# Three gather buffers instead of two beside the gate spreading, and later token rows for the second set

## The chip, the cores and the metric

The kernel runs on one core of one Trainium2 chip. The metric is device time in microseconds (us) for one execution of the whole program, taken as the median of several runs. All arithmetic is in float32.

## The reference, cut to what matters

One layer of a decoder trunk is computed for 256 tokens of width 2048. A mixer comes first. The change touches what follows it, the PEER retrieval. For each token, 8 heads pick 16 experts each out of 16,384, and every expert is one row of a table `u` and one row of a table `v`:

```python
def block(args):
    xb, idb, gb = args                      # tokens, expert numbers, gates
    ub = jnp.take(u_tab, idb, axis=0)
    act = jax.nn.gelu(jnp.einsum('tkd,td->tk', ub, xb))
    vb = jnp.take(v_tab, idb, axis=0)
    return jnp.einsum('tk,tkd->td', (gb * act), vb)
```

So a token needs 128 dot products with rows of `u` and a weighted sum of 128 rows of `v`. Each table holds 128 MB.

## The kernel before

The 256 tokens are split. For the last 160 tokens the kernel works densely: it multiplies their rows with the whole of both tables, and an array `p0` of gates (zero for experts not picked) selects what counts. For the first 96 tokens it gathers only the rows that were picked.

**The dense part.** TensorE multiplies 128 chunks of `u` (1 MB each, ring `wraw` of four slots, loaded by SyncE; function `chunk`, line L511), ScalarE takes the gelu of each result into `act_u` (L1063), and after that TensorE multiplies 128 blocks of `v` (1 MB each, eight slots: `wraw` and `vmore`, `v_tile`, L794). A chunk or block is 16 matmuls of 160 columns. In the trace each of these matmuls shows as two records, so a chunk is `x32`.

**The gate spreading.** `p0` is built beside chunks 20 to 47 of `u`. For each group of four tokens, 40 groups in all, VectorE writes one-hot matrices (`one_hots`, L1512 and L1516) into a ring of three (`HOT_RING`), TensorE multiplies them (`spread`, L771), and ScalarE copies the result into `p0` (`gates_out`, L1093). A chunk has one spread in its middle, and 12 of the 28 chunks have a second one at their end. TensorE runs its program in order, so a one-hot matrix that is late holds up the chunks behind it.

**The gathered part.** The 96 tokens form three sets of 32. Each take gathers one row for each of 32 tokens times four picks, 128 rows of 8 KB, 1 MB in all, by an indirect DMA that GpSimd issues (L1650). VectorE then uses it: a `u` take multiplies it with the token rows `hrep[:, s]` and sums (L1527), a `v` take adds it, weighted, to `yacc` (L1538). There are 192 takes of 32 each, in the order u0, u1, v0, u2, v1, v2. Gather buffers are the tiles `gat`. Beside the spreading two are in use. The third and fourth lie where the dense part holds the activations until then, and open when six batches of weights are done (`s_p0`).

**Order on VectorE.** Beside the spreading, `S0_TAKES` takes are dealt evenly behind the 40 groups of one-hots. Then come 16 batches `weights(i)` (L1545), each of which waits for eight chunks of `u` and is followed by `U_TAKES[i]` takes. The remaining takes come beside the `v` blocks. From take `G2_TAKE` = 136 on, every third one is followed by `add_g2`, which multiplies one of 16 modulation tiles that ScalarE's queue loads. The fourteenth of those loads stands behind a wait for 90 `v` blocks.

**Token rows.** `hrep` holds for each set the 32 tokens' rows, four times over (8 KB in each of 128 partitions for a set). It is written by four DMAs from `hrow_dram` that GpSimd issues: two sets before the takes begin (L1636), the third set when the spreading is done (L1645), since the one-hots lie in its place until then.

Of the kernel before, what the change touches and what calls it, by code (L numbers as in the profile page):

```python
# [37 lines left out]
D = 2048  # L38
# [38 lines left out]
SET_T = P // REP  # L77
# [3 lines left out]
N_TAKES = len(TAKES) * SET_G  # L81
# [6 lines left out]
GT = 4  # L88
SPREADS = N0 // GT
HOT_RING = 3  # L90
S0_TAKES = 36
U_TAKES = (0, 1, 0, 1, 0, 4) + (7, 7, 7, 7, 7, 6, 6, 5, 4, 4)
V_TAKES = N_TAKES - S0_TAKES - sum(U_TAKES)
G2_TAKE = 136
Y_BANKS = tuple(range(2, 8))
# [34 lines left out]
def hybrid_block(nc, xT, xrow, fnorm, par, cst, mixc, shifts, relb, wmod, wst, lruw, subk, sel, utab, vtab, hrow_dram, rel_dram, res_dram, silu_dram, gain_dram, out):  # L130
    ctx = ExitStack()
    with ctx:
# [9 lines left out]
        def at(name, kb, shape, dt=F32):  # L142
            assert kb * 256 + int(np.prod(shape)) <= size, name
            return nc.alloc_sbuf_tensor_at(name, [P, *shape], dt, offset=base + int(kb * 1024))
# [92 lines left out]
        hot_a = at("hot_a", 189.5, [HOT_RING, GT, P])  # L237
        hot_b = at("hot_b", 213.5, [HOT_RING, GT, P])
        p0 = at("p0", 77.5, [NB, N0])
        gat = [at(f"gat{i}", kb, [D]) for i, kb in enumerate((197.5, 205.5, 61.5, 69.5))]  # L240
        vmore = [at(f"vmore{i}", kb, [D]) for i, kb in enumerate((45.5, 53.5, 157.5, 165.5))]

        csil_back = at("csil_back", 77.5, [D])
# [78 lines left out]
        def v_slot(m):  # L322

            j = m % V_RING
            return row_of(wraw, (N_U + j) % W_RING) if j < W_RING else vmore[j - W_RING][:]

        def gather_slot(g):

            if g < S0_TAKES:
                return g % 2, (g // 2 + 1) * 16, (g - 2 if g >= 2 else None)  # L330
            slot, turn = (g - S0_TAKES) % 4, (g - S0_TAKES) // 4
            if slot < 2:
                return slot, (S0_TAKES // 2 + turn + 1) * 16, (g - 4 if turn else g - 2)
            return slot, (turn + 1) * 16, (g - 4 if turn else None)

        def taken(g):

# [19 lines left out]
        s_m0 = [sem(f"first_mod_loaded{i}") for i in range(M_RING0)]  # L357
        s_m = [sem(f"mod_loaded{i}") for i in range(M_RING)]
        s_v = [sem(f"v_loaded{i}") for i in range(V_RING)]
        s_gat = [sem(f"rows_gathered{i}") for i in range(4)]  # L360
        s_spill, s_back = sem("x1_stored"), sem("x1_loaded")
        s_dve, s_act = sem("dve_steps"), sem("act_steps")
        s_ones, s_silu_e, s_lam = sem("ones_set"), sem("silu_exp"), sem("lambda_steps")
# [801 lines left out]
        def _(dve):  # L1165
# [353 lines left out]
            def take(g):  # L1519

                kind, s_, k = taken(g)
                slot, count, _ = gather_slot(g)
                if kind == "u":
                    if k == 0:
                        dve.wait_ge(s_hrep, 64 if s_ < 2 else 128)
                    dve.wait_ge(s_gat[slot], count)
                    V.scalar_tensor_tensor(gat[slot][:], gat[slot][:], 1.0, hrep[:, s_], ALU.mult, ALU.mult,  # L1527
                                           accum_out=dots[:, s_, k:k + 1]).then_inc(s_used, 1)
                    return
                if k == 0:  # L1530
                    dve.wait_ge(s_pact, s_ + 1)
                    dve.wait_ge(s_used, g)
                    own.did(V.tensor_tensor(pact[:, s_], pact[:, s_], gate_rep[:, s_], ALU.mult))
                    own.did(V.memset(yacc[:, s_], 0.0)); own.settle()
                dve.wait_ge(s_gat[slot], count)
                if k:
                    dve.wait_ge(s_used, g)
                V.scalar_tensor_tensor(yacc[:, s_], gat[slot][:], pact[:, s_, k:k + 1], yacc[:, s_], ALU.mult,  # L1538
                                       ALU.add).then_inc(s_used, 1)
# [72 lines left out]
        def _(pool):  # L1612
# [20 lines left out]
            pool.wait_ge(s_hrowd, 16)  # L1633
            by_set = hrow_dram.rearrange("(s t) d -> t s d", t=SET_T)
            for r_ in range(REP):
                pool.dma_start(hrep[r_ * SET_T:(r_ + 1) * SET_T, 0:2], by_set[:, 0:2]).then_inc(s_hrep, 16)  # L1636

            pool.wait_ge(s_gidx, REP)
            for g in range(N_TAKES):
                kind, s_, k = taken(g)  # L1640
                slot, _, held = gather_slot(g)
                if g == S0_TAKES:
                    pool.wait_ge(s_gmm, SPREADS)
                    for r_ in range(REP):
                        pool.dma_start(hrep[r_ * SET_T:(r_ + 1) * SET_T, 2], by_set[:, 2]).then_inc(s_hrep, 16)  # L1645
                if held is not None:
                    pool.wait_ge(s_used, held + 1)
                elif g >= S0_TAKES:
# [104 lines left out]
```

## Time and profile before

| | |
|---|---|
| median of 3 runs | 1893.58 us (1893.5 to 1895.4) |
| the profiled execution's own time | 1891.61 us |
| span of its trace | 1889.8 us |
| TensorE busy | 1762.6 us, 93% of the span |
| VectorE busy | 1064.3 us, 56% |
| bytes moved | 672.99 MB, mean 356 GB/s |
| mean granted TensorE clock | 0.984 |

The span runs from the first to the last instruction. The profiled execution took 1.8 us more than its span. Matmul records are pipelined and a busy share near 100% only says that TensorE had no gap that the trace shows. Idle time of an engine that does not set the end costs nothing.

### The profile page before, as it was taken

The numbers are of one execution on the slowest core, as the hardware profiler recorded it, in microseconds if no ns is written. First come the engines' busy times: TensorE is split into PE (matmuls) and PEld (weight loads), VectorE is DVE, ScalarE is ACT, GpSimd is POOL, SyncE is SP. The second block draws the span as 40 slices with busy tenths as digits, with TensorE's granted clock in tenths as the row PEclk, the third lists the DMA queues.
The fourth block names the chain that finished last, engine by engine and source line by source line (L and its number), as shares of the span: only waits on it lengthen the run. The fifth ranks groups of instructions, "written<-read, shape, count | busy, mean of one in ns | idle before, by whom it ended". The sixth has DMA issues, their size and how long they took to land.

```text
span 1889.8 us, 26620 instructions
## 1 busy us (share of the span) xinstructions
PE 1762.6 (93%) x11476; PEld 1664.3 (88%) x11476; DVE 1064.3 (56%) x1396; ACT 259.1 (14%) x487; POOL 253.5 (13%) x211
## 2 busy tenths in 40 slices
PE   8999999998999988889999999999988888899997
PEld 6888888877999988889988899999888878899996
DVE  6668574685868777774555543254445555404512
ACT  2012401535522111110000000000000000000002
POOL 0000000000000012212222132121112222202200
PEclk9999999999999999989999999999998899999999
DMA  9999897586448789989999999999999999999971
GB/s 391 422 420 416 338 308 315 204 348 254 173 162 281 265 340 339 364 342 359 422 422 422 421 420 421 381 410 421 421 421 421 421 421 421 421 377 422 420 255 45
DMA packets 95517, 672.99 MB, mean 356 GB/s; under 512 B 12608, under 2 KB 13040, under 8 KB 14816
## 3 DMA queue, kind: packets, MB, share of 16 engines
q1 hardware_dynamic: 51072, 366.46, 48.5%
q0 software_dynamic: 29040, 208.50, 27.5%
q10 hardware_dynamic: 15312, 96.68, 13.2%
q8 instruction: 72, 1.18, 0.3%
q14 instruction: 21, 0.17, 0.0%
HBM read 665.41 MB, written 6.18 MB: 355 GB/s over the span
## 4 chain that ended last, share of the span: by engine, by line
PE 53%; DMA 40%; DVE 5%; ACT 1%; issue 1%; SPq 0%; ACTq 0%; DVEq 0%
PE ps L511 25%; PE ps L794 17%; DMA wraw<-vtab 17%; DMA wraw<-wst 11%; DMA gat<-utab,gidx 7%; DMA mod_first<-wmod 6%; DVE gat L1527 2%; PE ps L500 1%; PE ps L501 1%; PE ps L502 1%; PE ps L650 1%; PE ps L651 1%; PE ps L652 1%; DVE mod_first L1217 1%; PE ps L808 1%
## 5 line engine op out<-in xcount | busy, mean ns | idle before, releaser
L511 PE MATMUL ps<-h,wraw 128*128 128x160 f32 (+1 forms) x4160 | 590.9, 302 | 20.6 <-DMA wraw<-wst 9.7
L511 PEld LDWEIGHTS ps<-h,wraw 128*128 128x128 f32 x4160 | 573.5, 191 | 32.1 <-ACT act_u L1063 13.8
L1538 DVE SCALAR_TENSOR_TENSOR yacc<-gat,pact,yacc 128x2048 f32<-128x2048 f32 x96 | 225.6, 2349 | 202.9 <-DMA gat<-vtab,gidx 201.5
L1527 DVE SCALAR_TENSOR_TENSOR gat<-gat,hrep 128x2048 f32<-128x2048 f32 x96 | 219.6, 2291 | 198.0 <-DMA gat<-utab,gidx 198.0
L794 PE MATMUL ps<-p,wraw 128*128 128x160 f32 x2048 | 297.5, 307 | 30.5 <-DMA wraw<-vtab 30.5
L794 PEld LDWEIGHTS ps<-p,wraw 128*128 128x128 f32 x2048 | 289.2, 196 | 38.0 <-DMA wraw<-vtab 38.0
L794 PE MATMUL ps<-p,vmore 128*128 128x160 f32 x2048 | 291.7, 304 | 18.8 <-DMA vmore<-vtab 18.8
L794 PEld LDWEIGHTS ps<-p,vmore 128*128 128x128 f32 x2048 | 284.4, 193 | 24.7 <-DMA vmore<-vtab 24.6
L1650 POOL DMA_INDIRECT gat<-vtab,gidx x96 | 137.1, 1428 | 469.6 <-DVE yacc L1538 434.7
L511 PE MATMUL ps<-hid,wraw 128*128 128x256 f32 x832 | 180.7, 379 | 0.0
L511 PEld LDWEIGHTS ps<-hid,wraw 128*128 128x128 f32 x832 | 157.9, 190 | 21.0
L1650 POOL DMA_INDIRECT gat<-utab,gidx x96 | 106.7, 1112 | 473.9 <-DVE gat L1527 363.2
L1217 DVE SCALAR_TENSOR_TENSOR mod_ring<-mod_ring,csil_row 128x2048 f32<-128x2048 f32 x58 | 131.3, 2287 | 22.6 <-DMA mod_ring<-wmod 22.6
L547 PE MATMUL ps<-hid,wraw 128*128 128x256 f32 x512 | 114.1, 386 | 5.4 <-ACT hid L879 5.3
L547 PEld LDWEIGHTS ps<-hid,wraw 128*128 128x128 f32 x512 | 98.7, 194 | 21.0 <-issue 4.1
L1063 ACT ACTIVATE act_u<-ps 128x160 f32<-128x160 f32 x128 | 38.9, 304 | 470.3 <-PE ps L511 466.5
L1568 DVE SCALAR_TENSOR_TENSOR g_ring<-g_ring,csil_back 128x2048 f32<-128x2048 f32 x16 | 36.6, 2285 | 71.8 <-DMA g_ring<-wmod 71.8
L1142 ACT ACTIVATE ysb<-ps 128x480 f32<-128x480 f32 (+1 forms) x6 | 3.2, 527 | 494.1 <-PE ps L794 494.1
L771 PE MATMUL ps<-hot_b,hot_a 128*128 128x128 f32 x320 | 45.9, 288 | 25.2 <-DVE hot_b L1516 25.2
L1545 DVE TENSOR_TENSOR p<-act_u,p 128x1280 f32<-128x1280 f32 x16 | 23.6, 1487 | 80.5 <-ACT act_u L1063 80.5
L771 PEld LDWEIGHTS ps<-hot_b,hot_a 128*128 128x128 f32 x320 | 41.0, 198 | 29.3 <-DVE hot_b L1516 29.3
L1217 DVE SCALAR_TENSOR_TENSOR mod_first<-mod_first,csil_row 128x2048 f32<-128x2048 f32 x22 | 50.3, 2291 | 26.9 <-DMA mod_first<-wmod 26.8
(264 smaller groups left out, 1376.6 us busy)
## 6 DMA issues: line engine op xcount, KB each, us to landing
wraw<-wst SPq DMA_DIRECT2D x131, 1024.0 KB, 10.1
wraw<-wst ACTq DMA_DIRECT2D x71, 1024.0 KB, 8.0
wraw<-vtab SPq DMA_DIRECT2D x64, 1024.0 KB, 32.8
vmore<-vtab SPq DMA_DIRECT2D x64, 1024.0 KB, 31.9
mod_ring<-wmod SPq DMA_DIRECT2D x58, 1024.0 KB, 11.0
mod_first<-wmod SPq DMA_DIRECT2D x22, 1024.0 KB, 20.0
g_ring<-wmod ACTq DMA_DIRECT2D x16, 1024.0 KB, 12.5
x<-xT SPq DMA_DIRECT2D x4, 512.0 KB, 5.5
```

What stands on the lines that cost most here:

```text
L500: mm(dst, hi, src_hi, start=first, stop=False)
L511: r = mm(ps_w[k % 2][:, 0:T - low], wraw[:, j, kk, :], src[:, kk, low:T], start=(kk == 0), stop=(kk == KD - 1))
L547: r = mm(ps_acc[c], wraw[:, kk % W_RING, c, :], hid[:, kk, :], start=(kk == 0 and c % 2 == 0), stop=(kk == KD - 1), skip_group_check=True)
L771: r = mm(ps_spread[r_][:, t, :], hot_a[:, r_, t, :], hot_b[:, r_, t, :], start=True, stop=True)
L794: return mm(ps_y[kk], v_slot(m)[:, kk * P:(kk + 1) * P], p0[:, m, :], start=(m == 0 and kk % 3 == 0), stop=(m == NB - 1), skip_group_check ...
L1063: A(act_u[:, act_slot(b), :], ps_u[b % 2], ACT.Gelu_apprx_tanh).then_inc(s_wev, 1)
L1217: V.scalar_tensor_tensor(tile, tile, 1.0, csil_row[:], ALU.mult, ALU.mult, accum_out=mod_sum[:, m:m + 1]).then_inc(s_modacc, 1)
L1527: V.scalar_tensor_tensor(gat[slot][:], gat[slot][:], 1.0, hrep[:, s_], ALU.mult, ALU.mult, accum_out=dots[:, s_, k:k + 1]).then_inc(s_used, 1)
L1538: V.scalar_tensor_tensor(yacc[:, s_], gat[slot][:], pact[:, s_, k:k + 1], yacc[:, s_], ALU.mult, ALU.add).then_inc(s_used, 1)
L1545: V.tensor_tensor(p0[:, blocks, :], act_u[:, held:held + BATCH, :], p0[:, blocks, :], ALU.mult).then_inc(s_p0, 1)
L1568: V.scalar_tensor_tensor(g2_ring[slot][:], g2_ring[slot][:], 1.0, csil_back[:], ALU.mult, ALU.mult, accum_out=mod_sum[:, M_G2 + m:M_G2 + m ...
L1650: pool.indirect_dma_start(out=gat[slot][:], out_offset=None, in_=utab if kind == "u" else vtab, in_offset=bass.IndirectOffsetOnAxis(ap=gid ...
```

## The change

The takes beside the spreading go from 36 to 32, which is exactly set 0 of `u`. They use three buffers in turn instead of two. The third one, `gat4`, lies in the place of `hrep` of set 1. For that reason set 1's token rows are not loaded before the takes begin but together with set 2's, at the end of the spreading, and GpSimd now waits there for the 32 takes also. The batches of weights behind the spreading have the same 66 takes among them, placed a little later (none behind the batches 0 to 2, one each behind 3 and 4, four behind 5). Four takes more are left for the stretch beside the `v` blocks: 94 instead of 90.

```diff
-S0_TAKES = 36
-U_TAKES = (0, 1, 0, 1, 0, 4) + (7, 7, 7, 7, 7, 6, 6, 5, 4, 4)
+S0_TAKES = 32
+S0_SLOTS = (0, 1, 4)
+LATER_SLOTS = (0, 1, 2, 3)
+U_TAKES = (0, 0, 0, 1, 1, 4) + (7, 7, 7, 7, 7, 6, 6, 5, 4, 4)
...
-        gat = [at(f"gat{i}", kb, [D]) for i, kb in enumerate((197.5, 205.5, 61.5, 69.5))]
+        gat = [at(f"gat{i}", kb, [D]) for i, kb in enumerate((197.5, 205.5, 61.5, 69.5, 181.5))]
...
+        gathers, last_in = [], {}
+        for g in range(N_TAKES):
+            slot = S0_SLOTS[g % len(S0_SLOTS)] if g < S0_TAKES else LATER_SLOTS[(g - S0_TAKES) % len(LATER_SLOTS)]
+            turn = sum(1 for other, _, _ in gathers if other == slot) + 1
+            gathers.append((slot, turn * 16, last_in.get(slot)))
+            last_in[slot] = g
+
         def gather_slot(g):
 
-            if g < S0_TAKES:
-                return g % 2, (g // 2 + 1) * 16, (g - 2 if g >= 2 else None)
-            slot, turn = (g - S0_TAKES) % 4, (g - S0_TAKES) // 4
-            if slot < 2:
-                return slot, (S0_TAKES // 2 + turn + 1) * 16, (g - 4 if turn else g - 2)
-            return slot, (turn + 1) * 16, (g - 4 if turn else None)
+            return gathers[g]
...
-                        dve.wait_ge(s_hrep, 64 if s_ < 2 else 128)
+                        dve.wait_ge(s_hrep, 64 if s_ == 0 else 128)
...
-                pool.dma_start(hrep[r_ * SET_T:(r_ + 1) * SET_T, 0:2], by_set[:, 0:2]).then_inc(s_hrep, 16)
+                pool.dma_start(hrep[r_ * SET_T:(r_ + 1) * SET_T, 0], by_set[:, 0]).then_inc(s_hrep, 16)
...
                 if g == S0_TAKES:
                     pool.wait_ge(s_gmm, SPREADS)
+                    pool.wait_ge(s_used, S0_TAKES)
                     for r_ in range(REP):
-                        pool.dma_start(hrep[r_ * SET_T:(r_ + 1) * SET_T, 2], by_set[:, 2]).then_inc(s_hrep, 16)
+                        pool.dma_start(hrep[r_ * SET_T:(r_ + 1) * SET_T, 1:3], by_set[:, 1:3]).then_inc(s_hrep, 16)
```

## Rows read from the trace of the kernel before

**Rows 1.** Windows by stage: busy us (instructions) per engine, granted clock, DMA share, GB/s.

```profile
661.00:852.00 191.00, 165.81 (x1214) 161.66 (x1215) 144.85 (x271) 31.81 (x67) 37.29 (x34) 0.97 0.91 344
852.00:1227.00 375.00, 359.23 (x2571) 349.85 (x2570) 169.35 (x112) 25.17 (x83) 85.02 (x70) 1.00 1.00 411
1227.00:1370.00 143.00, 137.92 (x988) 134.30 (x987) 69.72 (x60) 0.00 (x0) 30.92 (x29) 1.00 1.01 415
1370.00:1645.00 275.00, 232.15 (x1529) 223.39 (x1530) 144.10 (x80) 1.72 (x3) 67.94 (x48) 0.94 1.01 421
1645.00:1854.00 209.00, 207.59 (x1522) 206.63 (x1521) 56.31 (x32) 1.14 (x2) 22.69 (x13) 1.00 0.89 350
```

**Rows 2.** Who waited for whom in 661 to 852 us: total, times, longest.

```profile
DVE gat L1527 <- DMA gat<-utab,gidx: 46.2, 26, 4.4
PE ps L771 <- DVE hot_b L1516: 25.2, 17, 4.0
```

**Rows 3.** Groups by line in 661 to 852 us: busy, mean ns | idle before.

```profile
L1527 DVE SCALAR_TENSOR_TENSOR gat<-gat,hrep 128x2048 f32<-128x2048 f32 x36 | 82.4, 2290 | 46.2 <-DMA gat<-utab,gidx 46.2
```

**Rows 4.** Timeline of TensorE, the spreading's start, a slow spot and its end.

```profile
660.95 2.41 PE L511 MATMUL ps<-h,wraw 128*128 128x160 f32 x16 [0.74 <-issue]
...
664.09 4.51 PE L511 MATMUL ps<-h,wraw 128*128 128x160 f32 x32
668.44 1.05 PE L771 MATMUL ps<-hot_b,hot_a 128*128 128x128 f32 x8
669.33 4.51 PE L511 MATMUL ps<-h,wraw 128*128 128x160 f32 x32
...
807.04 2.07 PE L771 MATMUL ps<-hot_b,hot_a 128*128 128x128 f32 x8 [4.04 <-DVE hot_b L1516]
808.91 6.17 PE L511 MATMUL ps<-h,wraw 128*128 128x160 f32 x32
...
852.28 69.81 PE L511 MATMUL ps<-h,wraw 128*128 128x160 f32 x512
```

**Rows 5.** Timeline of VectorE: two groups of one-hots with no wait between.

```profile
660.77 0.69 DVE L1512 TENSOR_TENSOR hot_a<-cst_sb,picks 128x512 f32<-128x512 f32 x1 [12.40 <-ACT picks L1074]
661.38 1.11 DVE L1516 TENSOR_SCALAR hot_b<-cst_sb,picks 128x128 f32<-128x128 f32 x4
662.41 0.68 DVE L1512 TENSOR_TENSOR hot_a<-cst_sb,picks 128x512 f32<-128x512 f32 x1
```

**Rows 6.** DMA issues in 661 to 852 us: count, KB each, median us to landing.

```profile
wraw<-wst SPq DMA_DIRECT2D x28, 1024.0 KB, 7.2
gat<-utab,gidx POOLq DMA_INDIRECT x34, 8.1
```

**Rows 7.** The same in 905 to 1121 us.

```profile
wraw<-wst SPq DMA_DIRECT2D x44, 1024.0 KB, 15.0
gat<-vtab,gidx POOLq DMA_INDIRECT x23, 17.2
gat<-utab,gidx POOLq DMA_INDIRECT x18, 17.3
```

**Rows 8.** Windows of 20 and 6 us inside the spreading.

```profile
760.00:780.00 20.00, 20.00 (x155) 20.00 (x154) 15.73 (x29) 4.20 (x9) 4.17 (x4) 1.00 0.95 375
806.00:812.00 6.00, 4.96 (x20) 4.96 (x21) 5.38 (x13) 0.60 (x1) 1.32 (x2) 0.50 0.66 231
```

**Rows 9.** TensorE's timeline and a window beside the first load of token rows.

```profile
601.47 30.67 PE L511 MATMUL ps<-h,wraw 128*128 128x160 f32 x224 [2.41 <-DMA wraw<-wst]
...
590.00:595.00 5.00, 5.00 (x39) 5.00 (x38) 4.86 (x18) 0.56 (x2) 0.00 (x0) 1.00 1.02 229
```

**Rows 10.** GpSimd's timeline behind the spreading.

```profile
852.75 2.04 POOL L1645 DMA_DIRECT2D hrep<-hrow_dram  x4 [6.26 <-PE ps L771]
...
877.87 0.94 POOL L1650 DMA_INDIRECT gat<-utab,gidx  x1 [20.12 <-DVE p L1545]
```

**Rows 11.** VectorE's timeline behind the spreading: first take, seventh batch.

```profile
867.48 2.29 DVE L1527 SCALAR_TENSOR_TENSOR gat<-gat,hrep 128x2048 f32<-128x2048 f32 x1 [10.57 <-DMA gat<-utab,gidx]
...
901.61 1.49 DVE L1545 TENSOR_TENSOR p<-act_u,p 128x1280 f32<-128x1280 f32 x1
```

**Rows 12.** TensorE's timeline beside the `v` blocks: two spots.

```profile
1340.34 4.61 PE L794 MATMUL ps<-p,wraw 128*128 128x160 f32 x32 [0.31 <-DMA wraw<-vtab]
1345.31 4.61 PE L794 MATMUL ps<-p,wraw 128*128 128x160 f32 x32 [0.36 <-DMA wraw<-vtab]
...
1687.60 17.55 PE L794 MATMUL ps<-p,wraw 128*128 128x160 f32 x128
1704.99 17.55 PE L794 MATMUL ps<-p,vmore 128*128 128x160 f32 x128
```

**Rows 13.** VectorE's timeline: the fourteenth modulation tile, and the last work on `yacc`.

```profile
1718.48 2.29 DVE L1568 SCALAR_TENSOR_TENSOR g_ring<-g_ring,csil_back 128x2048 f32<-128x2048 f32 x1 [71.84 <-DMA g_ring<-wmod]
```

More of the change, by code:

```diff
@@ L359, in hybrid_block @@
         s_v = [sem(f"v_loaded{i}") for i in range(V_RING)]
-        s_gat = [sem(f"rows_gathered{i}") for i in range(4)]
+        s_gat = [sem(f"rows_gathered{i}") for i in range(5)]
         s_spill, s_back = sem("x1_stored"), sem("x1_loaded")
```

## The prediction

> **What bounds the kernel now.** I read the windows by stage first [rows 1]. Each engine's busy time, the granted clock and the GB/s stand there for the five stretches from the start of the gate spreading to the last `v` block. TensorE is the engine whose program sets the end, so in each stretch I look for its gaps and for who made them. In the last stretch it has next to none. In the middle three the DMA engines move 411 to 421 GB/s, and TensorE loses time to them: its pace beside the `v` blocks is 4.97 us a block where it waits for `vtab`, against 17.39 / 4 = 4.35 us where it does not [rows 12]. The first stretch, the spreading, is different. It has the lowest rate of all, 344 GB/s, and yet TensorE has gaps.
>
> The waits say why [rows 2]. VectorE waited 46.2 us for gathers, and TensorE waited 25.2 us for one-hots, which VectorE writes behind those takes in program order. VectorE is not too slow by itself: a group of one-hots takes 1.64 us (660.77 to 662.41) [rows 5] and a take 2.29 us [rows 3]. A gather lands 8.1 us after its issue [rows 6], and with two buffers the next gather into a buffer must wait until the take before has been worked on. The 36 takes go by at one per 191.3 / 36 = 5.3 us.
>
> How fast could TensorE go through the spreading? A chunk starts at 664.09, its spread ends before 669.33, so one chunk with one spread is 5.24 us. Of this 4.35 is the chunk (664.09 to 668.44) and 0.89 the spread [rows 4]. The stage has 28 chunks and 40 spreads: 28 x 4.35 + 40 x 0.89 = 157.4 us. It took from 660.95 to 852.28, 191.3 us. So 33.9 us is the most that can be had here. 25.2 of them are the waits. The rest is restarting after them and a low clock: behind the longest wait, 4.04 us, a spread took 2.07 instead of 1.05 us and a chunk 6.17 instead of 4.51 [rows 4], in a window whose granted clock was 0.50 (the 1.2 GHz level) [rows 8]. [...]
>
> **The spreading with three buffers and 32 takes.** VectorE's own need is 40 x 1.64 + 32 x 2.29 = 65.6 + 73.3 = 139 us, under 157.4. The bytes are 28 chunks and 32 gathers of 1.049 MB, 62.9 MB. At the 421 GB/s of the busiest stage [rows 1] they need 149 us, and three of the gathers are issued before the stage begins (two before). That is tight but fits: 62.9 MB in 157.4 us is 400 GB/s, less the three early ones 380 GB/s. With two buffers the window from 760 to 780 already shows TensorE without a gap at 375 GB/s, with four gathers issued in 20 us, 5.0 us each [rows 8]. What is needed now is one per 157.4 / 32 = 4.92 us, or 5.2 us when the three early ones are taken off. When gathers and weight loads both stand in line, each gets about half: 44 loads of weights and 41 gathers in 216 us, one per 4.9 and 5.3 us [rows 7], and 4.97 us for a `v` block [rows 12], which I take for both. A chunk is needed only every 157.4 / 28 = 5.6 us, so the weight loads keep up even when every gather is given its half: four slots times 5.6 us is 22 us against 15.0 us to landing [rows 7].
>
> The rule in the Trainium skill (DMA: Bandwidth & Descriptors, queues, rings and completion order) is that each DMA engine serves its queues in turn, packet by packet. By this rule a third gather in line does not raise the queue's share, it only keeps the queue from running dry. The stage would then need 32 x 4.97 = 159 us. The rows of the crowded stretch agree with equal shares.
>
> So nearly the whole 33.9 us should be had. I leave 4 us for the unevenness of gathers and take 161 us: -30. The bounds of this term are -34 (no gap) and -21 (the old 5.3 us for each take, 32 x 5.3 = 170).
>
> **The first load of token rows.** It is cut from 2 MB to 1 MB. Such a load is costly: beside it the DMA engines were busy all the time but moved 229 GB/s, and TensorE waited 2.41 us for a chunk at 601.47 [rows 9]. The wait stands on TensorE's path, as VectorE's picks were ready about 12 us before they were asked for (its idle time before the first one-hots is 12.40 us [rows 5]). With half the load the wait should go: -2.4, bounds 0 and -2.6.
>
> **Behind the spreading.** Here 2 MB of token rows are loaded instead of 1 MB. Before, the four DMAs went out at 852.75, the first take behind them started at 867.48, 10.57 us of it VectorE's wait, the buffers three and four opened at 877.87, and the seventh batch of weights began at 901.61 [rows 10, 11]. Now GpSimd also waits for the 32nd take, a few us at most since that take stands right behind the last one-hots, the two gathers stand behind twice the load, and buffers three and four open only behind batch 5. I expect the first take 4 to 7 us later, counted from the end of the spreading, and the buffers 3 to 6 us later. What is queued behind VectorE's wait are batches 4 and 5. They are not urgent: TensorE does not read `p0` for another 350 us, and the activations' slots are not reused before batch 6 is needed at chunk 72, over 100 us on. GpSimd's extra wait has only gathers behind it. On TensorE the double load should make the same 2.4 us wait that it made at 601.47. The extra megabyte also takes 2.5 us of the DMA engines at 421 GB/s, or 4.6 us at 229, in a stretch that is full (411 GB/s); the stretch from 1121 on still has some slack. I take +3, bounds 0 and +7.
>
> **The four takes that move.** 4 takes go from the spreading to the stretch beside the `v` blocks. There the gathers have the DMA engines at one per 4.97 us, and TensorE goes at 4.97 instead of 4.35 us for a block. Four takes more keep this going for 4 x 4.97 = 19.9 us longer, and TensorE loses 0.62 in every 4.97 us: 2.5 us. The bound above is what four gathers need of a full DMA, 4 x 2.49 = 9.9 us; below, nothing. I take 2.5, because the gathers end long before TensorE does: VectorE stands idle for 71.84 us at 1718.48, waiting for a modulation tile whose load waits for 90 `v` blocks [rows 13]. The 20 us that VectorE comes later go into this idle time. If this cover were gone, each us would count at the end, since the last work on `yacc` follows the takes. It has over 45 us left.
>
> **The sum.** -30 - 2.4 + 3 + 2.5 = -27 us. It is made against the profiled execution, 1891.6 us with 1.8 us outside its span, which gives 1864.7. The median of the runs is 2.0 us above the profiled one: 1866.7, a gain of 1.4%. A difference within 0.2%, 3.8 us, I count as no change.
>
> **The rivals.**
> Gathers stay the bound (A). The rate of takes stays 5.3 us because a gather's time grows with the third in line, as landing grew from 8.1 to 17.3 us with four [rows 6, 7]. Then only the smaller number of takes helps: -21 - 2.4 + 3 + 2.5 = -18, 1876. For it: the gather share is near its limit. Against it: 5.0 us in the window at 760 with just two.
> The bytes are paid in full later (B). The spreading gains its 30, but everything behind it is DMA-bound, so the four gathers cost 9.9 and the larger load 7: -30 - 2.4 + 7 + 9.9 = -15.5, 1878. For it: 411 to 421 GB/s through 793 us. Against it: the last 209 us run at 350 GB/s without a gap on TensorE.
> The weight loads starve (C), the one on the other side. Gathers that always stand in line crowd out the chunks, TensorE waits for `wraw` inside the spreading, and the mean rate falls instead of rising, as it did to 229 GB/s at 590. It decides from the point where 62.9 MB take more than 188 us, that is below 334 GB/s. At 325 GB/s the stage takes 193.5 us: +2.2 - 2.4 + 3 + 2.5 = +5, 1899. Against it: the crowded stretches of these very two streams move 411 to 421 GB/s [rows 1].
> The change does not act (D): the third buffer is never the one missed and VectorE's waits are a matter of its order alone; that is A with other causes, and has its time.
>
> **Chances.** Forecast 0.70, A and D together 0.15, B 0.09, C 0.03, and 0.03 for something unseen that eats the gain. The likeliest case has its own range of 1859 to 1873: all bounds at their good ends give -36, 1857. With A and B it reaches 1880. Leaving out the very best end and C, I give 1858 to 1880. Faster by over 0.2%: 0.94, within 0.2%: 0.02, slower: 0.04.
>
> **What would show it.** In the changed kernel's trace the stretch from the first spread to the last should be 157 to 166 us long, with a rate of 380 to 400 GB/s instead of 344, TensorE's wait for one-hots under 8 instead of 25.2 us, and VectorE's wait for gathers well under 46.2 us. A gather should land in 10 to 13 us. The wait of 2.41 us at the first token rows should be gone, and one like it should show just behind the spreading. The first take behind the spreading should start about 20 us after it, not 15. The stretch of 4.97 us a block beside the `v` blocks should be 20 us longer, and VectorE's idle 71.84 us should be about 20 us shorter. The prediction is wrong if the spreading still takes over 170 us, if waits for `wraw` appear in it, or if the waits for `vtab` grow by more than 10 us.

## The result and the profile after

The changed kernel takes 1861.14 us, the median of 4 runs (1859.65 to 1862.37). The kernel before, run beside it, takes 1894.49 us (4 runs, 1893.5 to 1897.81). The ratio is 0.9819 with a 95% interval of 0.9803 to 0.9834: faster by 1.8%, 33 us between the medians. The prediction was 1866.7 us with a range of 1858 to 1880. Of the profiled executions, the one before took 1891.61 us (span 1889.8) and the one after 1861.16 us (span 1859.4): 30.4 us less, where the sum had said 27.

The changed kernel's lines are shifted by four or five: L515 is the chunk, L775 the spread, L798 the `v` block, L1531 the `u` take, L1549 the weights, L1655 the gather. First its windows by stage, with the columns of [rows 1]: spreading, the rest of `u`, and three parts of the `v` stretch.

```profile
659.00:817.00 158.00, 157.84 (x1219) 157.87 (x1220) 137.87 (x264) 31.93 (x68) 30.94 (x29) 1.00 0.96 390
817.00:1194.00 377.00, 358.97 (x2562) 348.99 (x2561) 167.24 (x111) 24.85 (x83) 83.34 (x70) 1.00 1.01 412
1194.00:1337.00 143.00, 137.99 (x991) 134.61 (x989) 69.66 (x58) 0.11 (x1) 31.16 (x29) 1.00 1.01 414
1337.00:1634.00 297.00, 248.67 (x1671) 237.62 (x1672) 155.39 (x88) 1.72 (x3) 72.22 (x52) 0.97 1.01 421
1634.00:1824.00 190.00, 188.51 (x1381) 187.55 (x1381) 54.67 (x31) 1.52 (x3) 22.17 (x13) 1.00 0.89 360
```

The spreading is 158 us long instead of 191, TensorE is busy in all of it, and the rate went from 344 to 390 GB/s. The fourth window is 22 us longer than its counterpart (297 against 275).

Who waited for whom in the spreading (659 to 817 us), with the columns of [rows 2]:

```profile
DVE hot_a L1516 <- PE ps L775: 9.9, 11, 1.3
DVE gat L1531 <- DMA gat<-utab,gidx: 4.0, 6, 1.3
```

TensorE's wait for one-hots is not in the list any more; it was 25.2 us [rows 2]. The order has turned round: VectorE now waits for TensorE, 9.9 us, because the ring of three one-hot matrices is full. Its wait for gathers fell from 46.2 to 4.0 us. The DMA issues of the same stretch, as [rows 6]:

```profile
wraw<-wst SPq DMA_DIRECT2D x28, 1024.0 KB, 9.3
gat<-utab,gidx POOLq DMA_INDIRECT x29, 10.7
```

Each gather takes longer to land, 10.7 instead of 8.1 us, and it no longer matters, since another one is ready.

TensorE's timeline at both ends of the spreading, and the first waits behind it, as [rows 4]:

```profile
659.16 2.41 PE L515 MATMUL ps<-h,wraw 128*128 128x160 f32 x16 [0.74 <-issue]
...
815.78 1.05 PE L775 MATMUL ps<-hot_b,hot_a 128*128 128x128 f32 x8
816.67 17.55 PE L515 MATMUL ps<-h,wraw 128*128 128x160 f32 x128
836.04 4.62 PE L515 MATMUL ps<-h,wraw 128*128 128x160 f32 x32 [1.82 <-DMA wraw<-wst]
841.10 52.78 PE L515 MATMUL ps<-h,wraw 128*128 128x160 f32 x384 [0.44 <-ACT act_u L1067]
```

From 659.16 to 816.67 it is 157.5 us. GpSimd behind the spreading, as [rows 10]:

```profile
817.13 2.20 POOL L1650 DMA_DIRECT2D hrep<-hrow_dram  x4 [17.67 <-PE ps L775]
...
848.58 0.94 POOL L1655 DMA_INDIRECT gat<-utab,gidx  x1 [25.94 <-DVE p L1549]
```

And VectorE there, and at the fourteenth modulation tile, as [rows 11, 13]:

```profile
839.69 2.29 DVE L1531 SCALAR_TENSOR_TENSOR gat<-gat,hrep 128x2048 f32<-128x2048 f32 x1 [16.50 <-DMA gat<-utab,gidx]
...
1688.81 2.29 DVE L1572 SCALAR_TENSOR_TENSOR g_ring<-g_ring,csil_back 128x2048 f32<-128x2048 f32 x1 [54.81 <-DMA g_ring<-wmod]
```

### The profile page after: what moved, and what is told of

Its sections match the earlier page's. It is cut to its first block, busy times and chain, and to the rows that moved or that the text cites. A ratio compares the mean times of both kernels' runs of the same rounds, so it can differ in the third digit from the quotient of the medians.

```text
span 1859.4 us, 26621 instructions
## 1 busy us (share of the span) xinstructions
PE 1752.4 (94%) x11476; PEld 1655.6 (89%) x11476; DVE 1064.7 (57%) x1396; ACT 258.9 (14%) x487; POOL 250.2 (13%) x211
## 4 chain that ended last, share of the span: by engine, by line
PE 61%; DMA 35%; DVE 2%; ACT 1%; SPq 0%; issue 0%; ACTq 0%; DVEq 0%
PE ps L515 32%; DMA vmore<-vtab 19%; PE ps L798 15%; DMA wraw<-wst 10%; DMA mod_first<-wmod 6%; PE ps L775 2%; PE ps L505 1%; PE ps L504 1%; PE ps L506 1%; PE ps L654 1%; PE ps L656 1%; PE ps L655 1%; DVE mod_first L1221 1%; PE ps L812 1%; DVE wlo L1381 0%; PE ps L523 0%
## 5 line engine op out<-in xcount | busy, mean ns | idle before, releaser
L515 PE MATMUL ps<-h,wraw 128*128 128x160 f32 (+1 forms) x4160 | 589.1, 302 | 20.4 <-ACT act_u L1067 9.4
L515 PEld LDWEIGHTS ps<-h,wraw 128*128 128x128 f32 x4160 | 571.1, 190 | 32.4 <-ACT act_u L1067 14.8
L1531 DVE SCALAR_TENSOR_TENSOR gat<-gat,hrep 128x2048 f32<-128x2048 f32 x96 | 219.8, 2290 | 184.5 <-DMA gat<-utab,gidx 184.5
L798 PE MATMUL ps<-p,vmore 128*128 128x160 f32 x2048 | 293.5, 304 | 29.9 <-DMA vmore<-vtab 29.9
L798 PEld LDWEIGHTS ps<-p,vmore 128*128 128x128 f32 x2048 | 284.5, 193 | 37.9 <-DMA vmore<-vtab 37.9
L798 PE MATMUL ps<-p,wraw 128*128 128x160 f32 x2048 | 292.0, 304 | 25.0 <-DMA wraw<-vtab 25.0
L798 PEld LDWEIGHTS ps<-p,wraw 128*128 128x128 f32 x2048 | 283.9, 193 | 32.1 <-DMA wraw<-vtab 32.1
L1655 POOL DMA_INDIRECT gat<-vtab,gidx x96 | 136.7, 1424 | 461.1 <-DVE yacc L1542 425.1
L515 PE MATMUL ps<-hid,wraw 128*128 128x256 f32 x832 | 180.7, 380 | 0.0
L515 PEld LDWEIGHTS ps<-hid,wraw 128*128 128x128 f32 x832 | 158.0, 190 | 20.9
L1655 POOL DMA_INDIRECT gat<-utab,gidx x96 | 103.9, 1082 | 443.4 <-DVE gat L1531 328.3
L1572 DVE SCALAR_TENSOR_TENSOR g_ring<-g_ring,csil_back 128x2048 f32<-128x2048 f32 x16 | 36.6, 2285 | 54.8 <-DMA g_ring<-wmod 54.8
L1549 DVE TENSOR_TENSOR p<-act_u,p 128x1280 f32<-128x1280 f32 x16 | 23.6, 1488 | 74.2 <-ACT act_u L1067 67.5
L504 PE MATMUL ps<-h_hi,chi 128*128 128x256 f32 x224 | 64.6, 288 | 0.0
L506 PE MATMUL ps<-h_hi,wlo 128*128 128x256 f32 x224 | 63.5, 283 | 0.0
```

The source lines that it names most:

```text
L504: mm(dst, hi, src_hi, start=first, stop=False)
L506: return mm(dst, lo, src_hi, start=False, stop=last)
L515: r = mm(ps_w[k % 2][:, 0:T - low], wraw[:, j, kk, :], src[:, kk, low:T], start=(kk == 0), stop=(kk == KD - 1))
L798: return mm(ps_y[kk], v_slot(m)[:, kk * P:(kk + 1) * P], p0[:, m, :], start=(m == 0 and kk % 3 == 0), stop=(m == NB - 1), skip_group_check ...
L1572: V.scalar_tensor_tensor(g2_ring[slot][:], g2_ring[slot][:], 1.0, csil_back[:], ALU.mult, ALU.mult, accum_out=mod_sum[:, M_G2 + m:M_G2 + m ...
L1655: pool.indirect_dma_start(out=gat[slot][:], out_offset=None, in_=utab if kind == "u" else vtab, in_offset=bass.IndirectOffsetOnAxis(ap=gid ...
```

## The stages of every run

To compare the kernels I cut each profiled execution at three instructions of TensorE: the first and the last spread, the first `v` block, and the first use of `yacc` (L808 before). What follows the last cut was 35.9 to 36.0 us in all of them. "Takes" are those beside the spreading, in the batches, and beside the `v` blocks. The first spread starts at 663.2 us before and at 661.4 after. The stages come from one execution of each kernel. Executions of one kernel differ by 1.6 to 11 us as a whole, and the two traces of one and the same kernel, e9 and e12, differ by up to 1.0 us in a stage. A stage that differs by 1 us or so between two kernels is therefore no finding.

```
run                           takes      first   spreading  u rest  v blocks  span     median
                                         spread
before                        36/66/90   663.2   189.0      374.1   627.6     1889.8   1894.5
after                         32/66/94   661.4   155.2      377.0   629.8     1859.4   1861.1
e1_two_buffers_32_takes       32/66/94   663.8   176.8      373.6   629.3     1879.5   1881.3
e2_two_buffers_rows_moved     32/66/94   659.6   171.9      380.4   628.9     1876.8   1882.5
e3_set2_rows_later            32/66/94   660.0   155.1      379.3   629.1     1859.5   1861.3
e4_four_takes_in_late_batches 32/70/90   658.8   155.2      383.2   627.2     1860.3   1863.0
e5_28_takes                   28/66/98   658.7   155.1      377.1   639.3     1866.1   1869.1
e6_v0_second_36_takes         36/66/90   660.3   166.0      379.0   626.2     1867.4   1866.4
e7_set2_rows_left_out         32/66/94   659.8   155.2      373.6   629.1     1853.7   1855.7
e8_62_takes_in_batches        32/62/98   659.1   155.1      375.8   640.3     1866.2   1868.1
e9_set1_rows_early            32/66/94   659.7   155.1      375.3   629.6     1855.6   1858.2
e10_early_rows_batches_first  32/66/94   659.7   155.2      379.0   628.1     1858.0   1861.3
e11_98_takes_late_residual    32/62/98   662.6   155.1      377.0   643.7     1874.4   1873.2
e12_set1_rows_early_again     32/66/94   660.7   155.1      376.0   628.8     1856.6   1859.2
```

Before to after, the spans differ by -1.8 (up to the first spread) -33.8 (spreading) +2.9 (the rest of `u`) +2.2 (`v` blocks) +0.1 (tail and rounding) = -30.4 us.

## Experiments

**Two buffers, 32 takes.** Is it the third buffer, or only that there are fewer takes?

```diff
 (kernel before)
-S0_TAKES = 36
-U_TAKES = (0, 1, 0, 1, 0, 4) + ...
+S0_TAKES = 32
+U_TAKES = (0, 0, 0, 1, 1, 4) + ...
```

> The kernel before with only the numbers of takes changed: 32 beside the spreading (two buffers, token rows of two sets loaded first, as before), 94 beside the v blocks. Theory (the third buffer does most of it): a take still needs 5.3 us with two buffers, so the spreading goes from 191.3 to about 170 us, and the four moved takes cost 2.2: about 19 us faster than before, near 1875. Rival (four takes fewer would have been enough): the spreading falls to 157.5 us as in the changed kernel, 31 us faster, near 1863.

Measured: 1881.27 us, ratio 0.9934 (0.991 to 0.9959). The spreading took 176.8 us, 12.2 less than before and 21.6 more than after. That is 176.8 / 32 = 5.5 us a take, as slow as before or a little slower. Its waits in the spreading:

```profile
DVE gat L1527 <- DMA gat<-utab,gidx: 42.2, 24, 5.0
PEld ps L771 <- DVE hot_b L1516: 16.4, 7, 4.0
PE ps L771 <- DVE hot_b L1516: 14.7, 6, 3.7
```

VectorE still waits 42.2 us for gathers. The rival is out: only about a third of the gain in the spreading, 12.2 of 33.8 us, comes with the four takes fewer. The theory's 170 us was too low for two buffers.

**Two buffers, rows moved.** The same two buffers, with the token rows of set 1 loaded late as in the changed kernel.

```diff
 (changed kernel)
-S0_SLOTS = (0, 1, 4)
+S0_SLOTS = (0, 1)
```

> The changed kernel with two buffers beside the spreading; token rows of set 1 still loaded late. Against the run with two buffers and rows as before, the moved rows alone: theory -1.8 us ahead of the spreading and +3 behind it, so about 1 us slower than that run, near 1876, 14 to 15 us slower than the changed kernel. Rival (buffers do not matter): equal to the changed kernel, 1861.

Measured: 1882.49 us, ratio 0.9942 (0.9927 to 0.9957), 1.2 us slower than the run above and 21 us slower than the changed kernel. By stages it is not the small sum that I expected but two larger terms: first spread 4.2 us earlier, spreading 4.9 us shorter, and the rest of `u` 6.8 us longer. The profiled execution of this kernel took 1878.61 us and its median is 3.9 us higher, so these two terms can be partly chance. The intervals of the two runs overlap: a net cost of moving the rows can't be told from nothing.

Against the changed kernel this run differs by one line, the third buffer. VectorE waits 37.4 us for gathers in its spreading (659 to 832 us), where the changed kernel has 4.0:

```profile
DVE gat L1531 <- DMA gat<-utab,gidx: 37.4, 20, 5.6
```

The spreading takes 171.9 us with two buffers and 155.2 with three. So the 33.8 us are made up of 12.2 (four takes fewer), 4.9 (token rows moved, by one trace each) and 16.7 (the third buffer).

**Fewer takes still.** The spreading has no gap left; what does a take cost beside the `v` blocks?

```diff
 (changed kernel)
-S0_TAKES = 32
+S0_TAKES = 28
```

> The changed kernel with 28 takes beside the spreading and 98 beside the v blocks. The spreading has no gap on TensorE already. Theory (beside the v blocks a take only prolongs the stretch of 4.97 us a block): spreading 155.2 us from first to last spread as before, v stretch 2.2 to 2.5 us longer, so 1863 to 1864. Rival (a gather costs its full DMA time there): 9.9 us longer, 1871.

Measured: 1869.05 us, ratio 0.9873 (0.9856 to 0.9889). The spreading stayed at 155.1 us, so it is TensorE's own time. But the `v` stretch grew by 9.5 us, the rival's number. Between 90 and 94 takes it had grown by 2.2.

**Takes moved between the batches and the `v` blocks.** Four more in the late batches, and four fewer.

```diff
 (changed kernel; the last ten of U_TAKES)
-(7, 7, 7, 7, 7, 6, 6, 5, 4, 4)
+(7, 7, 7, 7, 7, 7, 7, 5, 5, 5)      # e4: 70 in the batches, 90 later
+(7, 7, 7, 7, 6, 5, 5, 4, 4, 4)      # e8: 62 in the batches, 98 later
```

> The changed kernel with four more takes behind the batches 12 to 15 than before, so 90 instead of 94 beside the v blocks. Theory (a take costs 0.6 us where TensorE goes at DMA pace, nothing where the DMA has slack): the v stretch is 2.2 us shorter, the u stretch at most 1 us longer: 1 to 2 us faster than the changed kernel, 1859 to 1860. Rival (bytes cost the same anywhere): no change.

> The changed kernel with 62 instead of 66 takes behind the 16 batches, so 98 beside the v blocks. Four more in the batches had made the u stretch 6.2 us longer and the v stretch 2.6 us shorter. Theory (the same slope the other way): u stretch 4 to 6 us shorter, v stretch 2.2 to 2.6 longer, 2 to 3 us faster than the changed kernel, 1858 to 1859. Rival (the u stretch has slack once four gathers are gone and TensorE is its bound): u stretch at most 2 us shorter, no gain, 1861.

Measured: 1863.0 us (ratio 0.9844, 0.9817 to 0.9871) and 1868.06 us (0.9861, 0.9845 to 0.9878). With four more in the batches the `v` stretch gave back 2.6 us, as expected, but the rest of `u` grew by 6.2. With four fewer the rest of `u` shrank by just 1.2 us and the `v` stretch grew by 10.5. So the split of the changed kernel is at a knee on both sides: a gather costs 0.6 us from 90 to 94 beside the `v` blocks and 2.4 to 2.6 us from 94 to 98; in the batches it costs 0.3 us from 62 to 66 and 1.6 us from 66 to 70. Neither theory had such a knee. Both theories had forecast a gain over the changed kernel, and both kernels are slower than it, by 1.9 and 6.9 us between the medians.

What happens at 98? TensorE's timeline of that kernel late in the `v` stretch:

```profile
1663.68 4.61 PE L798 MATMUL ps<-p,wraw 128*128 128x160 f32 x32 [0.37 <-DMA wraw<-vtab]
1669.57 4.61 PE L798 MATMUL ps<-p,wraw 128*128 128x160 f32 x32 [1.27 <-DMA wraw<-vtab]
1676.35 4.61 PE L798 MATMUL ps<-p,vmore 128*128 128x160 f32 x32 [2.17 <-DMA vmore<-vtab]
...
1724.77 8.96 PE L798 MATMUL ps<-p,vmore 128*128 128x160 f32 x64 [0.35 <-DMA vmore<-vtab]
```

The changed kernel in the same place:

```profile
1643.39 4.62 PE L798 MATMUL ps<-p,vmore 128*128 128x160 f32 x32 [0.36 <-DMA vmore<-vtab]
1648.37 8.96 PE L798 MATMUL ps<-p,vmore 128*128 128x160 f32 x64 [0.36 <-DMA vmore<-vtab]
1657.16 17.55 PE L798 MATMUL ps<-p,wraw 128*128 128x160 f32 x128
```

There the last wait ends at 1648.37; with 98 takes the last one ends at 1724.77. In both, no gathers are made while VectorE stands idle for the fourteenth modulation tile, 54.8 us in one and 35.7 in the other. In that pause the weight loads have the DMA engines nearly alone (in the changed kernel 421 GB/s from 1645 to 1690 us). TensorE uses up 1.049 MB in 4.39 us there (17.55 / 4), 239 GB/s, so the ring of eight slots fills. Behind block 90 come the gathers again, with 6 MB of other loads. By an estimate from these numbers, the surplus of 182 GB/s fills eight slots, 8.4 MB, in 46 us. The kernel before had a pause longer than that, and its DMA engines did run short of work 33 to 53 us into the pause; in the changed kernel, as far into its pause, they did not (DMA share and GB/s are the last two columns; before, then changed):

```profile
1680.00:1700.00 20.00, 20.00 (x150) 20.00 (x149) 0.00 (x0) 0.00 (x0) 0.00 (x0) 1.00 0.88 316
1667.00:1687.00 20.00, 20.00 (x149) 20.00 (x149) 0.00 (x0) 0.00 (x0) 0.00 (x0) 1.00 1.01 421
```

So with 90 takes there was DMA time to spare in the pause, and with 94 none shows. That fits the knee: a further gather has to be paid with nearly its whole DMA time, 2.49 us.

**Residual rows later.** To test whether it is the burst behind block 90 that hurts, the 98 takes again with 3 MB less at its start.

```diff
 (62 takes in the batches; ScalarE's queue)
                 if m == KD - 4:
                     act.wait_ge(s_vmm, p0_free(133.5))
-                    act.dma_start(x2[:], res_dram).then_inc(s_back, 16)
-                    act.dma_start(fnrow[:], fnorm.to_broadcast([P, D])).then_inc(s_fn, 16)
+            act.dma_start(x2[:], res_dram).then_inc(s_back, 16)
+            act.dma_start(fnrow[:], fnorm.to_broadcast([P, D])).then_inc(s_fn, 16)
             act.wait_ge(s_vmm, p0_free(143))
```

> The kernel with 62 takes in the batches and 98 beside the v blocks (v stretch 640.3 us, 10.5 longer than with 94), but the 3 MB of the residual rows and the last norm's row are loaded behind the last three modulation tiles instead of ahead of them. Theory (with 98 takes the gathers stop too shortly before block 90 for the ring of v blocks to fill again, and the burst behind block 90 then stalls TensorE between 1669 and 1725 us): with 3 MB less in the burst's beginning part of these waits goes, v stretch 633 to 637 us, 1861 to 1865. Rival (every gather beside the v blocks costs its 2.5 us of DMA time, and the burst has no part in it): v stretch stays within 1 us of 640.

Measured: 1873.18 us, ratio 0.9886 (0.9869 to 0.9902), and a `v` stretch of 643.7 us, 3.4 longer. My theory of the burst missed. The edit had a side that I had not priced: the modulation tile came sooner, so VectorE's pause was 23.8 instead of 35.7 us:

```profile
1678.78 2.29 DVE L1572 SCALAR_TENSOR_TENSOR g_ring<-g_ring,csil_back 128x2048 f32<-128x2048 f32 x1 [23.78 <-DMA g_ring<-wmod]
```

Set side by side, the pause and the `v` stretch go together: 71.8 us and 627.6 (before), 70.2 and 626.2 (e6), 67.8 and 627.2 (e4), 54.8 and 629.8 (after), 35.7 and 640.3 (e8), 34.2 and 639.3 (e5), 23.8 and 643.7 (e11). The seven other runs with 94 takes lie with the changed kernel: pauses of 52.8 to 54.2 us, `v` stretches of 628.1 to 629.6. That fits that the pause in the gathers is what refills the ring, and that it is long enough down to about 55 us. The pause was not tried alone: between most of these runs the number of takes changes with it, and e11, which holds the takes against e8, moves 3 MB of loads as well. So it stays an explanation that agrees with the runs, not one that they show.

**Set 2's rows later, and left out.** What are the +2.9 us in the rest of `u`?

```diff
 (e3: changed kernel; GpSimd, LATE_ROWS = 76; VectorE's waits for the rows follow suit)
-                        pool.dma_start(hrep[r_ * SET_T:(r_ + 1) * SET_T, 1:3], by_set[:, 1:3]).then_inc(s_hrep, 16)
+                        pool.dma_start(hrep[r_ * SET_T:(r_ + 1) * SET_T, 1], by_set[:, 1]).then_inc(s_hrep, 16)
+                if g == LATE_ROWS:
+                    for r_ in range(REP):
+                        pool.dma_start(hrep[r_ * SET_T:(r_ + 1) * SET_T, 2], by_set[:, 2]).then_inc(s_hrep, 16)
```

```diff
 (e7: changed kernel; VectorE and GpSimd)
-                    V.scalar_tensor_tensor(gat[slot][:], gat[slot][:], 1.0, hrep[:, s_], ALU.mult, ALU.mult,
+                    V.scalar_tensor_tensor(gat[slot][:], gat[slot][:], 1.0, hrep[:, min(s_, 1)], ALU.mult, ALU.mult,
...
-                        pool.dma_start(hrep[r_ * SET_T:(r_ + 1) * SET_T, 1:3], by_set[:, 1:3]).then_inc(s_hrep, 16)
+                        pool.dma_start(hrep[r_ * SET_T:(r_ + 1) * SET_T, 1], by_set[:, 1]).then_inc(s_hrep, 16)
```

> The changed kernel, but at the end of the spreading only set 1's rows (1 MB) are loaded, set 2's stand in front of gather 76. Theory (the double load makes TensorE's 1.8 us wait for a chunk just behind the spreading and is most of the +3 us there): the wait goes, the stretch up to the first v block is 1 to 3 us shorter, 1858 to 1860. Rival (the stretch is bound by bytes, wherever they go): the same time within 1 us, 1861, and the wait turns up around gather 76.

> The changed kernel, but set 2's u takes use set 1's token rows, and set 2's rows are never loaded: 1 MB less behind the spreading, nothing else. This kernel computes other dot products for set 2. Theory (the u stretch is bound by bytes and the extra megabyte is its whole growth from 374.1 to 377.0): u stretch back at 374 to 374.5 us, TensorE's wait of 1.8 us just behind the spreading gone, 1858. Rival (the growth is from VectorE's later takes and gathers, which wait for the 32nd take and for batch 5): u stretch stays at 376 to 377.

Measured: 1861.29 us (ratio 0.9831, 0.9805 to 0.9857) and 1855.72 us (0.98, 0.9783 to 0.9816). Left out, the megabyte takes 3.4 us off the rest of `u`, 373.6 against 377.0, and the wait just behind the spreading is gone. Loaded later, the wait behind the spreading is gone too, but the megabyte costs more, 379.3, with its waits in the new place (TensorE's timeline of e3):

```profile
1051.86 4.58 PE L516 MATMUL ps<-h,wraw 128*128 128x160 f32 x32 [2.36 <-DMA wraw<-wst]
1059.61 4.61 PE L516 MATMUL ps<-h,wraw 128*128 128x160 f32 x32 [3.17 <-DMA wraw<-wst]
```

The extra megabyte is thus enough for the whole growth. But e7 does not take it out alone. In the changed kernel VectorE's first take comes 23 us behind the end of the spreading (839.69 - 816.67), where it had been 15. In e7 it comes 14 us behind it (829.48 - 815.07), as before the change:

```profile
829.48 2.29 DVE L1531 SCALAR_TENSOR_TENSOR gat<-gat,hrep 128x2048 f32<-128x2048 f32 x1 [7.88 <-DMA gat<-utab,gidx]
```

So the megabyte and the late take go away together, and e7 can't tell the theory from its rival. Two other runs help. Both load all the rows and have no late take: e3 (15 us behind the spreading) has 379.3, and e9, further down (6 us), has 375.3. The bytes therefore cost something without the late take; what the late take adds is, by these runs, at most the 1.0 to 1.7 us between the changed kernel and e9 or e12.

Nor is the stretch bound by its bytes as such. The kernel e8 has four gathers fewer in it, 4.2 MB, and gained 1.2 us; this one megabyte gave 3.4. Why token rows cost so much more for their size than gathers is taken up in the last section.

**v0 as second, 36 takes.** Can the spreading carry the old number of takes with three buffers?

```diff
 (changed kernel)
-TAKES = (("u", 0), ("u", 1), ("v", 0), ("u", 2), ("v", 1), ("v", 2))
-S0_TAKES = 32
+TAKES = (("u", 0), ("v", 0), ("u", 1), ("u", 2), ("v", 1), ("v", 2))
+S0_TAKES = 36
...                                    # the gelu of set 0's sums stands behind chunk 45 on ScalarE, that of set 1 behind the last chunk
```

> The changed kernel with the takes in the order u0, v0, u1, u2, v1, v2 and 36 of them beside the spreading, still with three buffers. The four that come behind set 0's u takes are v takes and need no token rows of set 1. Theory (VectorE stopped gathering 17 us ahead of the end of the spreading, and there is room for four more): spreading 155 to 158 us, v stretch 2.2 us shorter, and the first take behind the spreading no longer needs token rows: 1857 to 1860. Rival (the DMA engines have no room for four more gathers in 155 us): the spreading grows by 5 to 10 us and the kernel is 3 to 8 us slower than the changed one.

Measured: 1866.41 us, ratio 0.9851 (0.9834 to 0.9867), about 5 us slower than the changed kernel, with a spreading of 166.0 us (10.8 longer): about the rival's size. But not only for its reason. VectorE's timeline at the change from `u` to `v` takes:

```profile
809.24 0.19 DVE L1537 TENSOR_TENSOR pact<-pact,gate_rep 128x32 f32<-128x32 f32 x1 [3.91 <-ACT pact L1104]
809.81 1.76 DVE L1538 MEMSET yacc<- 128x2048 f32 x1 [0.38 <-issue]
```

VectorE waited 3.91 us for ScalarE's gelu, where I had put it, and then cleared `yacc`, in front of one-hots that TensorE wanted; TensorE waited 3.83 us for them. VectorE's waits for gathers were 15.0 us in all, against 4.0. How much would be left with the gelu placed better stays open. The theory also began from a misreading: the 17 us were not VectorE's. They are GpSimd's wait for the last spread, when all 32 gathers had been issued (17.67 us up to 817.13). VectorE did its last take at 808.59, and its wait at the end of the spreading was 6.61 us.

**Set 1's rows early.** In the changed kernel GpSimd stood 17.67 us waiting for the last spread, from 799.5 on, and the third buffer was done with for good at 802, so set 1's rows can go out there.

```diff
 (changed kernel; GpSimd, in front of gather 32; VectorE's waits for the rows follow suit)
                 if g == S0_TAKES:
+                    pool.wait_ge(s_used, S0_TAKES - 2)
+                    for r_ in range(REP):
+                        pool.dma_start(hrep[r_ * SET_T:(r_ + 1) * SET_T, 1], by_set[:, 1]).then_inc(s_hrep, 16)
+                if g == S0_TAKES + 2:
                     pool.wait_ge(s_gmm, SPREADS)
-                    pool.wait_ge(s_used, S0_TAKES)
                     for r_ in range(REP):
-                        pool.dma_start(hrep[r_ * SET_T:(r_ + 1) * SET_T, 1:3], by_set[:, 1:3]).then_inc(s_hrep, 16)
+                        pool.dma_start(hrep[r_ * SET_T:(r_ + 1) * SET_T, 2], by_set[:, 2]).then_inc(s_hrep, 16)
```

> The changed kernel, but set 1's token rows are loaded as soon as the third buffer is free for good (30 takes done), set 2's behind gather 33. In the changed kernel VectorE is 17 us ahead there, GpSimd waits 17.7 us for the last spread, and the first 38 us behind it run at 341 GB/s. Theory (a megabyte of rows and two gathers go into DMA time that stood empty, and buffers three and four open earlier): u stretch 377 falls to 370 to 374 us, the 16.5 us wait of VectorE for take 32 falls under 5, spreading stays 155: 3 to 6 us faster than the changed kernel, 1855 to 1858. Rival (the rows slow down the weight loads inside the spreading): spreading 2 to 4 us longer, no gain.

> The run with set 1's rows early once more, with more rounds, because its distance to the changed kernel (1858.2 against 1861.1) is not clear of what single runs differ by. Theory: ratio to the kernel before 0.979 to 0.981, u stretch 375 us. Rival (it was chance): ratio 0.982 or above, u stretch 377.

Measured: 1858.24 us, ratio 0.9806 (0.977 to 0.9843), and again 1859.18 us, ratio 0.9818 (0.9805 to 0.9832). VectorE's first take behind the spreading starts 6.6 us after it without a wait (in the second run after a wait of 1.32 us), and the spreading is not longer. But the rest of `u` is only 1.0 to 1.7 us shorter, 375.3 and 376.0 us. The medians are 2 to 3 us under the changed kernel's, and the ratios cannot be told from its 0.9819. If it is better, it is by 0.1%; this stays open.

**Batches first.** With that edit, and buffers three and four opened as early as can be. The batches 6 to 15 keep their takes.

```diff
-U_TAKES = (0, 0, 0, 1, 1, 4) + ...
+U_TAKES = (0, 0, 0, 0, 0, 6) + ...
```

> As the run with set 1's rows early, and the two takes behind batches 3 and 4 stand behind batch 5, so that the batches 0 to 5 follow each other with no take between and buffers three and four open about 9 us behind the last spread. Theory (what the stretch lost is DMA time that stands empty at its start, 38 us at 341 instead of 422 GB/s, 7 us): u stretch 368 to 372 us, 5 to 8 us faster than the changed kernel, 1853 to 1856. Rival (it is the bytes, not their start, and gathers that start earlier only take weight loads' time earlier): equal to the run with early rows alone within 1 us.

Measured: 1861.25 us, ratio 0.9822 (0.9787 to 0.9857). The first of the gathers that wait for batch 5 went out at 824.60, 9 us behind the last spread, as meant, and it did not help: the rest of `u` was 379.0 us. TensorE's timeline shows why:

```profile
830.96 6.26 PE L515 MATMUL ps<-h,wraw 128*128 128x160 f32 x32 [2.76 <-DMA wraw<-wst]
837.97 4.61 PE L515 MATMUL ps<-h,wraw 128*128 128x160 f32 x32 [0.75 <-DMA wraw<-wst]
843.81 4.58 PE L515 MATMUL ps<-h,wraw 128*128 128x160 f32 x32 [1.23 <-DMA wraw<-wst]
```

Token rows, gathers and weight loads now come all at once, and the first 38 us still run at 341 GB/s (in the changed kernel too, from 816.6 to 854.4 us):

```profile
816.00:854.00 38.00, 32.50 (x220) 31.38 (x219) 17.43 (x14) 2.12 (x7) 8.13 (x9) 0.96 1.01 341
```

The DMA engines are busy there (share 1.01), and they were in the changed kernel too (0.99). What I had read as empty DMA time is mostly the slow load of the token rows.

## Why the prediction was right, point by point

**The bound.** That the spreading was held by VectorE's waits for gathers, and that 157.4 us is TensorE's floor there, was right: 157.5 us measured, and 155.1 to 155.2 between the first and last spread in every kernel with three buffers and at most 32 takes.

**The spreading's term** is the one that was mis-sized: -30 forecast, -33.8 measured. I had left 4 us for unevenness of the gathers. There was none to pay, since VectorE had time in hand: it waited 9.9 us for TensorE inside the stage, and 6.61 us at its end. Its wait for gathers, 4.0 us, fitted into that. The stage moved 390 GB/s, within the 380 to 400 forecast, and gathers landed after 10.7 us (10 to 13 forecast). Rival A is out: the rate of takes rose, and with two buffers alone it did not. Rival C is out: no wait for `wraw` inside the stage. D is out by e2, which is the changed kernel without the third buffer: 16.7 us more in the stage and 21 us in all.

**The first token rows:** -2.4 forecast. The wait at 601.47 is gone, and the first spread came 1.8 us earlier in the pair of traces. Over all runs it started at 658.7 to 662.6 us with the small load (twelve traces, middle 659.8) and at 663.2 and 663.8 with the large one. So the pair may understate this term.

**Behind the spreading:** +3 forecast, +2.9 measured, and the wait of 2.41 us came back as one of 1.82. That the extra megabyte costs this much agrees with e7 (3.4 us). How well the two numbers meet is in part luck, as other places for the same megabyte gave 375.3 to 379.3 us. The forecast had said that nothing waits for the late batches. That was not shown, since in e7 VectorE is no longer late. The lateness itself was somewhat larger than forecast: the first take came 7.8 us later than before, counted from the end of the spreading (4 to 7 forecast), and buffers three and four opened 6.3 us later (3 to 6 forecast).

**The four moved takes:** +2.5 forecast, +2.2 measured, and about the same in the seven other runs with 94 takes (628.1 to 629.6 us against 626.2 to 627.6 with 90). The waits for `vtab` reached from 1300.6 to 1661.4 us before and reach from 1272.3 to 1648.4 after, 15 us longer where 20 were forecast. The reasoning was incomplete. I took VectorE's idle 71.84 us as cover of which over 45 us would be left after the change. 54.8 us are left, and the next four takes already cost 9.5 to 10.5 us, rival B's price. The time in which VectorE is idle was in use: the loads that fill the ring went on in it, at 421 GB/s. That the term came out right was therefore in part luck: the change stops just short of the knee. TensorE's waits for `vtab` rose from 49.3 to 54.9 us (wraw 30.5 + vmore 18.8; now 25.0 + 29.9), more than the stretch grew. The waits alone are a poor measure here, since the granted clock changes them. The kernel of e9 and e12 is the same, and its two `v` stretches had a clock of 1.00 and 0.98:

```profile
1190.10:1819.60 629.50, 568.88 (x4042) 552.21 (x4041) 279.74 (x176) 3.16 (x6) 126.05 (x94) 1.00 0.97 401
1191.80:1820.70 628.90, 577.46 (x4042) 563.61 (x4042) 279.69 (x176) 3.16 (x6) 125.75 (x94) 0.98 0.98 402
```

At the lower clock TensorE was busy 8.6 us longer and waited 9.2 us less for `vtab` (51.4 against 60.6), and the stretch was no longer. In this pair the slower clock cost nothing in a stretch whose pace the DMA sets.

**What would have made it wrong:** nothing of the list came about. The waits for `vtab` grew by 5.6 us, not by more than 10. The 27 us of the sum stand against 30.4 in the profiled pair and 33 between the medians; the rest is that the profiled execution before was 2.9 us under the median of its 4 runs.

## What to carry to other kernels

When one engine works in order on two streams, ask how long a buffer is away (issue, landing, use) and divide by the number of buffers: here 2 gave a take every 5.3 us, and 3 took the gather off the path although each landed later. Work out the floor of the engine that sets the end, instruction by instruction; it was met within 0.1 us, and an allowance for unevenness was not needed once the other engine had slack. And an idle time is not free cover only because the idle engine sets nothing: see what its silence lets others do, and count its price in steps, since the second four takes cost over four times the first. The remark ahead of the prediction that such idle time costs nothing holds for the idle engine's own time only.

## What was not expected of the hardware

The loads of token rows move slowly while the DMA engines count as fully busy. Four DMAs read the same rows of `hrow_dram` into four groups of partitions, and beside them the rate was 229 GB/s at a share of 1.02 [rows 9], against 421 to 422 GB/s at 1.01 in stretches with weight loads and gathers. With more in line it was no better: 341 GB/s over 38 us in e10, as in the changed kernel. Which part of it is slow, the repeated reads or the shape of the transfer, was not tried.
